# HGRN levels in half width, and the two widest levels copied out by ScalarE

## The reference, cut to what matters

```
b = jnp.cumsum(lf, axis=2)                        # log decay, negative steps
diff = b[:, :, :, None, :] - b[:, :, None, :, :]
decay = jnp.exp(jnp.where(causal[:, :, None], diff, NEG_BIG))
# score of query t and source s, s <= t:  sum over channels q[t] * k[s] * decay[t, s]
# out[t] = sum over s of score[t, s] * v[s]
```

## Time and profile before

| | us |
|---|---|
| median of three runs | 1531.72 |
| span of the profiled execution | 1527.0 |
| PE busy in it | 1477.4 (97%) |
| DVE busy | 811.7 (53%) |
| ACT busy | 573.6 (38%) |
| POOL busy | 317.6 (21%) |
| the stage of this change | 1043 to 1097 |

### The profile page before, as it was taken

How to read it: one execution, slowest core, us unless ns; L and a number is a source line. 1 busy time by engine, 2 the same in 40 slices (tenths; PEclk the granted TensorE clock), 3 DMA queues, 4 the chain that set the end, 5 groups by cost and what they waited for, 6 DMA issues and landing times. The chain is left out here.

```text
span 1527.0 us, 18721 instructions
## 1 busy us (share of the span) xinstructions
PE 1477.4 (97%) x7613; PEld 1203.3 (79%) x7613; DVE 811.7 (53%) x1122; ACT 573.6 (38%) x905; POOL 317.6 (21%) x304
## 2 busy tenths in 40 slices
PE   7999999999999999999999999999899999999998
PEld 5888787886788888888887776676778888888886
DVE  4232434578656537433355699878846434333425
ACT  4231534457635413223144532385434323112312
POOL 1000100000023897000002289634421000000000
PEclk9999999999999999999999999999999999999999
DMA  4231222220032323232332222110013323232322
GB/s 186 84 110 61 81 67 94 77 84 1 29 128 79 111 83 111 83 110 83 110 110 66 92 75 84 62 56 29 29 56 111 110 83 111 83 110 83 110 70 82
DMA packets 38858, 129.25 MB, mean 85 GB/s; under 512 B 4676, under 2 KB 23004, under 8 KB 27380
## 3 DMA queue, kind: packets, MB, share of 16 engines
q1 hardware_dynamic: 38484, 127.93, 24.4%
q10 hardware_dynamic: 288, 0.12, 0.0%
HBM read 124.82 MB, written 3.17 MB: 84 GB/s over the span
## 5 line engine op out<-in xcount | busy, mean ns | idle before, releaser
L266 PE MATMUL bank<-xT_hi,ring_hi 128*128 128x512 f32 (+2 forms) x928 | 355.2, 383 | 7.2 <-DVE xT_lo L1728 4.8
L266 PE MATMUL bank<-xT_hi,ring_lo 128*128 128x512 f32 (+2 forms) x928 | 351.7, 379 | 0.0
L266 PE MATMUL bank<-xT_lo,ring_hi 128*128 128x512 f32 (+2 forms) x928 | 351.6, 379 | 0.0
L247 DVE TENSOR_TENSOR ring_lo<-ring_raw,ring_hi 128x2048 fp32r<-128x2048 f32 (+3 forms) x112 | 260.2, 2325 | 168.8 <-ACT ring_hi L233 168.6
L233 ACT CAST ring_hi<-ring_raw 128x2048 fp32r<-128x2048 f32 (+4 forms) x114 | 211.0, 1852 | 240.6 <-DMA ring_raw<-in_w_ff 130.6
L266 PEld LDWEIGHTS bank<-xT_hi,ring_hi 128*128 128x128 f32 (+1 forms) x928 | 174.1, 188 | 47.9 <-issue 7.8
L266 PEld LDWEIGHTS bank<-xT_hi,ring_lo 128*128 128x128 f32 (+1 forms) x928 | 174.0, 187 | 33.9
L266 PEld LDWEIGHTS bank<-xT_lo,ring_hi 128*128 128x128 f32 (+1 forms) x928 | 174.1, 188 | 32.6
L266 PE MATMUL bank<-ring_hi,hid_hi 128*128 128x512 f32 x416 | 162.0, 390 | 0.0
L266 PE MATMUL bank<-ring_hi,hid_lo 128*128 128x512 f32 x416 | 161.9, 389 | 0.0
L266 PE MATMUL bank<-ring_lo,hid_hi 128*128 128x512 f32 x416 | 161.9, 389 | 0.0
(11 more groups left out here) (505 smaller groups left out, 2155.8 us busy)
## 6 DMA issues: line engine op xcount, KB each, us to landing
ring_raw<-in_w_ff SPq DMA_DIRECT2D x30, 1024.0 KB, 4.8
ring_raw<-in_w_up SPq DMA_DIRECT2D x22, 1024.0 KB, 4.8
ring_raw<-in_w_proj SPq DMA_DIRECT2D x8, 1024.0 KB, 5.1
ring_raw<-in_w_gates SPq DMA_DIRECT2D x8, 1024.0 KB, 4.9
ring_raw<-in_w_fm SPq DMA_DIRECT2D x12, 512.0 KB, 5.0
ring_raw<-in_w_dn_a SPq DMA_DIRECT2D x6, 1024.0 KB, 4.8
ring_raw<-in_w_proj SPq DMA_DIRECT2D x8, 512.0 KB, 4.5
ring_raw<-in_w_out SPq DMA_DIRECT2D x4, 1024.0 KB, 4.8
```

What stands on the lines that cost most here:

```text
L247: k.nc.vector.tensor_tensor(k.ring.lo[:, g % SLOTS, 0:n], k.raw[:, g % SLOTS, 0:n], plain(k.ring.hi[:, g % SLOTS, 0:n]), ALU.subtract).the ...
L266: mm = k.nc.tensor.matmul(out, x, y, start=first and n == 0, stop=last and n == 3 * len(pairs) - 1)
```

## The change

Three things change in `stage_recurrent`.

First, in the levels n = 1 to 64, PE's moving operand holds only the columns of the right halves: of the 128 queries of a token block, the 64 that lie in right halves, in runs of n columns with gaps of n. The four results of a head are 128x64 and fill the first half of its bank. The number of matmuls and the 128 weight columns stay.

Second, DVE's predicated copy of those levels reads these 256 columns, takes the right-half columns of the mask and writes the right-half columns of `hg_acc`. It runs over 256 elements for each partition, in runs of n.

Third, the copies of the two widest levels leave DVE. ACT makes them at the end of its queue, behind its two sigmoids, and counts them on a new semaphore `hg_wide`. PE's level 9 (n = 256) waits for it where it waited for DVE. The wait for POOL's `s5_low` goes along to ACT.

```diff
             def select(i, h):
...
                 elif n <= 64:
-                    mask = k.mask_lev[:, i, :].bitcast(mybir.dt.uint16).unsqueeze(1).to_broadcast([P, T, P])
-                    x = v.copy_predicated(rows(acc[:, h, :]), mask, rows(ps[:, :]))
-                elif n == 128:
-                    if h == 0:
-
-                        dve.wait_ge(s5_low.sem, s5_low.base + 1)
-                    x = v.tensor_copy(off[0][:, h, :, :], ps[:, 0:256].rearrange("p (c s) -> p c s", c=2))
-                else:
-                    x = v.tensor_copy(off[1][:, h, :, :], ps[:, :].rearrange("p (c s) -> p c s", c=4))
+                    m = P // (2 * n)
+                    mask = k.mask_lev[:, i, :].bitcast(mybir.dt.uint16).rearrange("p (b c h) -> p b c h", c=2, h=n)[:, :, 1, :]
+                    dst = acc[:, h, :].rearrange("p (t b c h) -> p t b c h", t=T, c=2, h=n)[:, :, :, 1, :]
+                    x = v.copy_predicated(dst, mask.unsqueeze(1).to_broadcast([P, T, m, n]),
+                                          ps[:, 0:S // 2].rearrange("p (t b h) -> p t b h", t=T, h=n))
                 x.then_inc(sel.sem, 1)
...
-                for h in range(4):
+                for h in range(4) if halves[i] <= 64 else ():
                     select(i, h)
...
             end.gates(act)
+            for i in (nl - 2, nl - 1):
+                for h in range(4):
+                    act.wait_ge(sc.sem, sc.base + 4 * i + h + 1)
+                    if i == nl - 2 and h == 0:
+
+                        act.wait_ge(s5_low.sem, s5_low.base + 1)
+                    dst, w = (off[0], 256) if i == nl - 2 else (off[1], S)
+                    nc.scalar.copy(dst[:, h, :, :], k.pb[h][:, 0:w].rearrange("p (c s) -> p c s", s=P)).then_inc(wide.sem, 1)
...
-                if n <= 64:
+                if i == 0:
                     blocks = [(t * P, t * P, P, t * P) for t in range(T)]
+                elif n <= 64:
+                    blocks = [(t * P, t * P, P // 2, t * P // 2) for t in range(T)]
...
-                    if i >= 1:
+                    if i == nl - 1:
+
+                        pe.wait_ge(wide.sem, wide.base + 2 * f + 2)
+                    elif i >= 1:
 
                         pe.wait_ge(sel.sem, sel.base + 4 * (i - 1) + 2 * f + 2)
...
-                            mm = nc.tensor.matmul(k.pb[2 * f + odd][:, c:c + w], L[:, s0:s0 + P], R[:, t0:t0 + w],
-                                                  start=True, stop=True, skip_group_check=True)
+                            out, moving = k.pb[2 * f + odd][:, c:c + w], R[:, t0:t0 + w]
+                            if 1 <= i and n <= 64:
+
+                                moving = R[:, t0:t0 + P].rearrange("p (b c h) -> p b c h", c=2, h=n)[:, :, 1, :]
+                                out = out.rearrange("p (b h) -> p b h", h=n)
+                            mm = nc.tensor.matmul(out, L[:, s0:s0 + P], moving, start=True, stop=True,
+                                                  skip_group_check=True)
```

More of the change, by code:

```diff
@@ L3219, in stage_recurrent @@
     made, ex, sc, sel = (k.sig(x) for x in ("hg_exponent", "hg_exp", "hg_scores", "hg_selected"))
-    zr = k.sig("hg_z")
+    zr, wide = k.sig("hg_z"), k.sig("hg_wide")
     dm, qk, dec, pp, mixed, outd, v1_made = (
@@ L3443, in _ @@
             fill(5, QK[0])
-    for s, n in ((made, nl - 1), (ex, nl - 1), (zr, nl - 1), (sc, 4 * nl), (sel, 4 * nl), (dm, 2 * steps),
+    for s, n in ((made, nl - 1), (ex, nl - 1), (zr, nl - 1), (sc, 4 * nl), (sel, 4 * (nl - 2)), (wide, 8), (dm, 2 * steps),
                  (qk, 2 * steps), (dec, 2 * steps), (pp, 2 * steps), (mixed, 4), (outd, 4), (v1_made, 2)):
```

## The result

The changed kernel takes 1552.88 us (median of four runs, 1543.63 to 1555.57) against 1530.74 us for the kernel before (median of four): a ratio of 1.0127 with a 95% interval of 1.0104 to 1.0150, so it is slower. The forecast was 1528.1 us. The profiled execution took 1555.21 us with a span of 1553.4 us, 26.4 more than before.

The account below looks back on a forecast made before the run. PE was taken to bound the kernel, nearly tied with DVE in this stage. Gains of 0.3, 1.06, 0.87, 0.2, 0.9 and 0.24 us made 3.6, taking 1531.7 to 1528.1 us; range 1524 to 1533.

Parts of the forecast that it names:

- rival 4: In the stage, likeliest levels 4 to 6, PE's clock falls: 1.7 us lost each, 1536.6 us with five; chance 0.10.
- Part 1, the selects: DVE's predicated copies at half width take 0.445 us each, four in 1.49: 1.07 us less per level, 7.5 over seven.
- levels 2 and 3: PE binds: DVE finishes selects before PE empties its queue, so PE's waits vanish there: 1.36 us ahead by the logs for ScalarE's decay.
- wait for ScalarE: PE's wait of 0.94 us for ScalarE's decay, behind the squares, grows to about 1.5 us.
- Part 2, the matmuls: Levels 1 to 7 at 64 columns gain only 0.1 us each, since something other than streaming sets the pace.
- g: Time by which one level's 32 matmul records get shorter at 64 columns: 0.1 us, bounds 0 and 0.9.
- Rival 1: In the narrowed levels columns set PE's pace, 0.9 us per level: 5.6 us gained in all, 1526.1 us; chance 0.10.
- Part 3, ScalarE's copies: Copies of the two widest levels move from DVE to ScalarE behind its sigmoids, taking 0.39 and 0.59 us.
- Level 9 waits for neither DVE nor ACT: ScalarE's copies of level 8 come in time, covered by PE's 0.95 us wait at level 8; without cover PE stands 0.9.
- Level 8, the hold behind POOL: DVE's multiply L3275 is held to the end of POOL's long operation, so PE waits about 0.95 us ahead of level 8.
- Rival 2: Ahead of the last mix POOL holds DVE's small multiply 2.3 us, giving back 1.75 of 3.6 us: 1529.9; chance 0.25.
- Rival 3: Selects don't get cheaper because of short runs; only about 1.4 us gained, 1530.3 us; chance 0.10.

Follow-up runs that it names:

- the pair of kernels above: Kernels with spread squares, early level 8 copies and seven fillings ahead of level 1: 128 columns (1527.94 us) against 64 in levels 1 to 7 (1527.11 us).
- squares spread: Changed kernel with 128-column products again and ScalarE's sixteen squares done four, four and eight in three turns instead of one: 1529.99 us, ratio 0.9989.
- the kernel of 1527.11 us: Changed kernel (64 columns in levels 1 to 7) plus ScalarE's squares in three turns, level 8 copies before its sigmoids, seven fillings ahead of level 1: ratio 0.9984.

## Why the prediction was wrong

**The sum of the forecast left the clock at 1.00, and the chip took rival 4.** The step that failed is the price and the chance of rival 4, *PE's clock falls*. I priced a fall at 1.7 us, from the one place in the earlier trace rows (the trace has a second fall as long, at 17.2), and let five falls cost 8.5. It fell once and stayed low for 64.9 us. I had set this rival at 0.10 and left its price outside the range. The 22.4 us by which the stage grew plus the 3.6 that the forecast had it gain (not measured) are 26.0 us, 0.40 us for each us at the lower level; the two rows behind the 1.7 give 0.5 by the share of the clock. So the price of a low microsecond was about right, and its length was wrong by a factor of 19. What I did not ask is what brings the clock back. In the earlier trace rows it came back while PE worked on full-height products of 512 columns; in the changed stage everything up to level 7 is thin, and even level 8 (128 columns) still ran low, until the clock came back 4.1 us behind the start of level 9. The evidence that I held against the rival, 985 to 990 us with PE busy 2.15 of 5 us at 1.00, was one stretch of five microseconds in which no fall happened to come: in the profile of the changed kernel and in those of eight experiments a fall of 3.4 to 6.8 us begins at 985.9 to 988.3, in the same code. A clock of 1.00 in one execution is not a margin.

The Trainium skill (TensorE: Matmul & The Clock Gate, "Terms") reckons the penalty of a throttled stretch at its length times the share of the clock that is lost; an estimate by that rule is 32.5 us for 64.9 us low. The runs agree in kind, with some 26.0; that the rest hid where PE would otherwise have waited fits the vanished waits, and is not shown by itself. The same page ("Loop structure matters more than you think") counts a DVE copy between matmuls as harmless to a warm PE. At 128 columns with the filling in its place the runs agree (1527.55 us with a wait of 0.83 us for DVE); the changed kernel's fall of 64.9 us began 2.4 us behind such a wait, and whether the wait caused it is open.

**Part 1, the selects: right from level 3 on, wrong for levels 1 and 2.** I had 0.445 us each and four in 1.49. Levels 3 to 7 measured 0.42 to 0.44 and 1.42 to 1.61. Runs of 1 and 2 columns measured 2.43 and 2.60 for four, at the other end of the bounds. The argument that L3276 has one price whatever its runs did not carry over to a predicated copy; whether its mask, its source or its output makes the difference was not tried. So the step *levels 2 and 3: PE binds* fell with it: at full clock PE still waits 0.27 and 0.18 us there with 128 columns. Most of the 1.36 that I had "ahead" at the squares was not to be had. The nearly equal wait for ScalarE (1.48 against 1.5) does not rescue this: it came out at the size forecast while the terms that I derived it from were off, and I did not separate the reasons.

**Part 2, the matmuls: right, and half as large.** I took 0.1 for g and bounded it by 0 and 0.9. Before, level to next instruction is 2.06 long and the next one starts 1.98 behind; now 1.93. That is 0.05 a level; over the whole stage, where PE also waits for DVE, it came to 0.15 us in the pair of kernels above. Rival 1, columns set the pace, is out. This should have weighed more than it did: an edit that removes half of PE's streaming and next to none of its time has no gain with which to pay for any risk.

**Part 3, ScalarE's copies: durations right, place wrong.** 0.38 and 0.59 us, as taken. *Level 9 waits for neither DVE nor ACT* failed in three of the four profiles that ran levels 7 and 8 at full clock with the changed order of ScalarE: 1.01 us in the kernel with more filling, whose level 8 had no wait of 0.95 in front to cover the sigmoids, 1.02 with 128 columns and 1.01 with 64 in level 1 alone. In the fourth (squares spread), where level 8 did wait 0.77, level 9 did not. This cover and its price of 0.9 were named, but the case was not given the chance it had.

**Level 8, the hold behind POOL: right.** L3275 lasted 1.58 us in the kernel with more filling, and in the six kernels that waited ahead of level 8 at full clock it lasted 2.46 to 2.53 us and PE's wait 0.76 to 0.88, against 0.95 forecast.

**Rivals 2 and 3.** Rival 2 (POOL holds DVE's small multiply) came true in all four of these profiles: 1.86, 2.01, 1.79 and 2.17 us on DVE. It reached PE as a wait of 1.37 us against 1.75 in one of them (squares spread); in the others level 9 was late for ScalarE anyway. Its 0.25 was too low. Rival 3 was true for two levels of seven.

**The span and the median.** The 4.7 us that I carried from the one to the other are some 1.8 us outside the span, as 1555.21 against 1553.4 shows, and some 2.9 of spread: the profiled execution of before was a fast one. The sum's 3.6 us don't hang on it.

**What stays open.** The changed kernel itself never ran with its clock up in four runs, so the 3.6 us of the forecast can't be read from it. The nearest is the kernel with early copies and spread squares at 64 columns (44.31 us from level 1 on, where before had 1097.13-1048.42 = 48.71): 4.4 us less, of which the part due to the two extra edits is not separated. Nor do the runs say why the same program at the same place falls in some runs and not in others; the two groups of the kernel with more filling show that it does, and no more. What would settle the part of the wait is the kernel of 1527.11 us and the one without its seven fillings, side by side on one chip.

## What to carry to other kernels

Before you remove work from an engine whose clock depends on its load, ask what that work was worth in time: here something other than the columns set the pace, half of them were worth 0.15 us, and with all of them the clock came back within 17.1 us of each fall in every profile. Price a clock fall by what follows it, not by the last fall you saw: here it was 3.4 us with wide products behind it and 64.9 with narrow ones, so look at what stands behind each wait. When a change makes one engine faster, list the waits that it makes longer on TensorE and remove those first; with that done (squares spread, copies ahead of the sigmoids, a few matmuls in the wait) the narrower selects and ScalarE's copies gave 1527.94 us with products of 128 columns, and 1526.32 with 64 in levels 5 to 7 alone. And before you lay a difference between two kernels with such a spread to the code, run both on one chip.

## What the runs showed of the hardware

- The granted clock went to its lower level once and stayed there for 64.9 us while PE was 100% busy with matmuls of 64 rows by 64 columns, mixes of 128 by 65, short scores and, near the end, a level of 128 and one of 256 columns (54.6 us in the kernel with narrow products alone, 47.8 with the front filled). With levels of 128 columns behind the fall it came back after 3.4 to 17.1 us.
- One program has two groups of times on one chip: six runs within 0.6 us of each other and four 11 to 21 us above. A single profile of either group would have told the wrong story; with 64 columns and the front wait, it was the one good run of five that was profiled.
- The clock fell at 1058.8 in one profile and held in another, though all engines had done the same things in the 9 us before, within about 0.02 us, but for four small squares on ScalarE.
- A predicated copy of 128x256 takes 0.42 to 0.44 us in runs of 4 columns and more; in runs of 1 and 2 four of them take 2.43 to 2.60 us, up to 0.80 each.
- A multiply of 128x4 on DVE lasted 2.01 us instead of 0.17 while POOL worked on 128x1024 elements (2.17 with the squares spread).
